# Half of each expert's down product as split operands, and one copy of the whole result

## What is computed

```python
D_MODEL, SEQ, DEPTH = 1024, 512, 2
N_EXPERTS, TOP_K_IN_GROUP, D_EXPERT = 16, 2, 256
for i in range(DEPTH):
    ...
    h = layer_norm_2(DN_ALPHA * h + mix, ln1_g[i], ln1_b[i])
    # two experts of 16 for every token: silu(h @ w1) * (h @ w3) @ w2, weighted by the router
    y_moe = hier_moe(h, moe_wgc[i], moe_bgc[i], moe_wgf[i], moe_bgf[i], moe_w1[i], moe_w3[i], moe_w2[i])
    y_ple = jax.nn.sigmoid(h @ ple_wg[i] + ple_bg[i]) * (p[i] @ ple_wp[i])
    h = layer_norm_2(DN_ALPHA * h + y_moe + y_ple, ln2_g[i], ln2_b[i])
```

## Time and profile before

| | us |
|---|---|
| median of three runs | 3018.23 (3017.04 to 3021.21) |
| the profiled execution, its own time | 3016.39 |
| its span in the trace | 3014.6 |
| PE busy over the span | 2853.4 (95%) |
| DVE busy | 1723.2 (57%) |
| POOL busy | 1538.0 (51%) |
| ACT busy | 1069.8 (35%) |

### The profile page before, as it was taken

The page is one execution under the profiler, slowest core; times in us unless marked ns, Lnnn a source line. Parts: engine busy times, 40 slices in busy tenths (PEclk is TensorE's granted clock), DMA queues, the critical chain, the costliest instruction groups (busy, mean ns, idle before and its releaser), DMA issues. The chain is left out here.

```text
span 3014.6 us, 36257 instructions
## 1 busy us (share of the span) xinstructions
PE 2853.4 (95%) x12934; PEld 2247.6 (75%) x12934; DVE 1723.2 (57%) x2416; ACT 1069.8 (35%) x1851; POOL 1538.0 (51%) x929
## 2 busy tenths in 40 slices
PE   8999999999999999999999999989999799899996
PEld 6778787888876787878888876677667567687774
DVE  5875645443137855554441266566777465667775
ACT  3533323221025333332220122524555314444563
POOL 4543366666764533476666654565225253672241
PEclk9999999999999999999999889999999899899998
DMA  4221122332332211223333222125982321246942
GB/s 150 76 63 56 57 72 83 97 97 94 95 98 70 77 57 50 63 80 95 97 97 106 63 96 64 47 88 188 346 331 106 117 76 50 69 177 232 358 164 84
DMA packets 87034, 338.28 MB, mean 112 GB/s; under 512 B 19952, under 2 KB 22768, under 8 KB 77936
## 3 DMA queue, kind: packets, MB, share of 16 engines
q1 hardware_dynamic: 67744, 303.33, 29.8%
q0 software_dynamic: 17280, 26.26, 2.5%
q10 hardware_dynamic: 1872, 6.82, 0.6%
HBM read 371.98 MB, written 30.41 MB: 133 GB/s over the span
## 5 line engine op out<-in xcount | busy, mean ns | idle before, releaser
L179 POOL TENSOR_SCALAR wh<-ring 128x1024 fp32r<-128x1024 f32 x337 | 371.7, 1103 | 1000.1 <-PE ps L240 779.4
L181 POOL TENSOR_TENSOR wl<-ring,wh 128x1024 fp32r<-128x1024 f32 x337 | 825.6, 2450 | 28.1
L238 PE MATMUL ps<-xh,wh 128*128 128x512 f32 x1720 | 695.4, 404 | 32.7 <-POOL xl L439 11.5
L239 PE MATMUL ps<-xl,wh 128*128 128x512 f32 x1720 | 673.9, 392 | 0.0
L240 PE MATMUL ps<-xh,wl 128*128 128x512 f32 x1720 | 673.9, 392 | 0.0
L238 PEld LDWEIGHTS ps<-xh,wh 128*128 128x128 f32 x1720 | 325.5, 189 | 123.8 <-issue 38.4
L239 PEld LDWEIGHTS ps<-xl,wh 128*128 128x128 f32 x1720 | 326.0, 190 | 70.9 <-issue 6.3
L240 PEld LDWEIGHTS ps<-xh,wl 128*128 128x128 f32 x1720 | 325.3, 189 | 69.6
L1434 DVE SCALAR_TENSOR_TENSOR taps<-ps,par,taps 128x511 f32<-128x511 f32 x192 | 143.9, 749 | 237.0 <-ACT taps L1174 222.2
L2793 DVE TENSOR_TENSOR ew_l<-ew,ew_h 128x1024 fp32r<-128x1024 f32 x184 | 219.2, 1252 | 0.0
L2381 ACT ACTIVATE ew_h<-ew 128x1024 fp32r<-128x1024 f32 x184 | 179.3, 1050 | 0.0
(11 more groups left out here) (501 smaller groups left out, 5161.2 us busy)
## 6 DMA issues: line engine op xcount, KB each, us to landing
ring<-in_w SPq DMA_DIRECT2D x343, 512.0 KB, 3.6
ew<-in_eu SPq DMA_DIRECT2D x32, 2048.0 KB, 9.9
ew<-in_ed SPq DMA_DIRECT2D x32, 1024.0 KB, 9.4
yg<-ypicks SPq DMA_DIRECT2D x16, 512.0 KB, 7.1
xrows<-xr ACTq DMA_DIRECT2D x8, 512.0 KB, 2.6
z<-in_x SPq DMA_DIRECT2D x4, 512.0 KB, 4.5
gw<-in_gw SPq DMA_DIRECT2D x2, 1024.0 KB, 6.5
out<-z SPq DMA_DIRECT2D x8, 256.0 KB, 2.9
```

Source lines behind the costliest of these rows:

```text
L179: nc.gpsimd.tensor_scalar(hi, raw, 1.0, 0.0, ALU.mult, ALU.add).then_inc(sem["w_hi"], 1)
L181: nc.gpsimd.tensor_tensor(lo, raw, hi, ALU.subtract).then_inc(sem["w_split"], 1)
L238: nc.tensor.matmul(out, wh, xh, start=first, stop=False, **kw)
L239: nc.tensor.matmul(out, wh, xl, start=False, stop=False, **kw)
```

## The change

From the third tile of each layer on (`DN_FROM = 2`), the block f = 0 of the down matrix, and the hidden activations that it meets, are split: ACT copies the block's high part into `down_h` (128x1024), DVE subtracts it from the block in place, and DVE also splits the hidden activations into `hidT_h` and `hidT_l` (128x128 each). PE then multiplies that block with `three` instead of with a plain float32 product; block f = 1 stays plain and now comes first. `down_h` is one buffer, so ACT fills it for tile j only when the down product of tile j-1 is finished. The result of a tile, both halves, is now copied by ACT in one instruction of 128x1024, once both banks are finished (`dn_mm`); DVE no longer copies any of it. Only the last tile keeps two copies, both on ACT. On ACT, part 3 of the next tile's high weights now stands ahead of that copy.

```diff
@@ -1468,6 +1468,7 @@
 NOWHERE = 8192
 UP_PARTS = EW_UP // D
 HI_SLOTS = 7
+DN_FROM = 2
 V_POOL = 0
 HY_ORDER = (2, 4, 3, 5, 0, 1)
 HY_EARLY = 4
...
@@ -1571,6 +1572,9 @@
         sil = at_("sil", 152, [P, DE])
         hact = at_("hact", 153, [P, DE])
         hactT = at_("hactT", 154, [P, EC, P])
+        hidT_h = at_("hidT_h", 154, [P, P], F32R)
+        hidT_l = at_("hidT_l", 155, [P, P], F32R)
+        down_h = at_("down_h", 172, [P, D], F32R)
         xr = at_("xr", 156, [P, 4, D])
         xg = at_("xg", 156, [P, 2, D])
         ew_l = at_("ew_l", 80, [P, EW_BUFS, EW_UP + EW_DOWN], F32R)
...
@@ -1613,7 +1617,7 @@
                  "router_ready", "logit_mm", "logits", "route_mm", "r_max", "r_exp", "picks", "rank_mm", "slot_mm", "slots", "spare_ready", "idx_ready", "half_ready2",
                  "rt_in", "xrow_mm", "xrow_evac", "xrow_out", "xg_in0", "xg_in1", "xgt_mm", "xgt_lo", "xgt_hi",
                  "ew_up0", "ew_up1", "ew_up2", "ew_dn0", "ew_dn1", "ew_dn2", "es_up0", "es_up1", "es_dn0", "es_dn1", "e_hi", "e_lo", "up_mm", "silu", "hact", "hactt_mm", "hactt",
-                 "dn_half", "dn_mm", "y_lo", "y_hi", "y_out0", "y_out1", "yg_in0", "yg_in1", "yg_in2", "yg_in3", "zt_mm", "zt_taken",
+                 "dn_half", "dn_mm", "d_hi", "d_lo", "y_done", "y_out0", "y_out1", "yg_in0", "yg_in1", "yg_in2", "yg_in3", "zt_mm", "zt_taken",
                  "tk_mean", "tk_sq", "tk_std", "tk_norm", "xt_mm", "pg_sig", "pp_done", "pt_hi", "pt_lo", "pq_mm", "pq_evac", "stored", "in_rstd", "in_rows", "consts"])
         sem, sem_range = sems(nc, ctx, names)
 
...
@@ -2161,19 +2164,25 @@
                     def expert_down(j):
 
                         b = j % EW_BUFS
-                        pe.wait_ge(sem["hactt"], at("hactt", j + 1))
+                        pe.wait_ge(sem["hactt"], at("hactt", 2 * j + (1 if j >= DN_FROM else 2)))
                         if j < EXPERTS:
                             pe.wait_ge(sem[f"ew_dn{b}"], at(f"ew_dn{b}", 16 * (j // EW_BUFS + 1)))
                         else:
                             k = j - EXPERTS
                             pe.wait_ge(sem[f"es_dn{k % 2}"], at(f"es_dn{k % 2}", 16 * (k // 2 + 1)))
                         if j:
-                            pe.wait_ge(sem["y_lo"], at("y_lo", j))
-                            pe.wait_ge(sem["y_hi"], at("y_hi", j))
+                            pe.wait_ge(sem["y_done"], at("y_done", j))
                         for half in range(2):
-                            for f in range(EC):
-                                a_ = EW_UP + f * D + half * S
-                                mm = T.matmul(ps[:, 5 + half, :], hactT[:, f, :], ew[:, b, a_:a_ + S], start=(f == 0), stop=(f == EC - 1))
+                            a_ = EW_UP + half * S
+                            T.matmul(ps[:, 5 + half, :], hactT[:, 1, :], ew[:, b, a_ + D:a_ + D + S], start=True, stop=False)
+                            if j < DN_FROM:
+                                mm = T.matmul(ps[:, 5 + half, :], hactT[:, 0, :], ew[:, b, a_:a_ + S], start=False, stop=True)
+                            else:
+                                if half == 0:
+                                    pe.wait_ge(sem["hactt"], at("hactt", 2 * j + 2))
+                                    pe.wait_ge(sem["d_lo"], at("d_lo", j - DN_FROM + 1))
+                                mm = three(nc, ps[:, 5 + half, :], hidT_h[:, :], hidT_l[:, :], down_h[:, half * S:half * S + S],
+                                           ew_l[:, b, a_:a_ + S], False, True)
                             mm.then_inc(sem["dn_mm" if half else "dn_half"], 1)
 
                     for j in range(TILES):
...
@@ -2189,9 +2198,7 @@
 
                     for c in range(4):
                         if c == 2:
-                            pe.wait_ge(sem["y_lo"], at("y_lo", TILES))
-                        if c == 3:
-                            pe.wait_ge(sem["y_hi"], at("y_hi", TILES))
+                            pe.wait_ge(sem["y_done"], at("y_done", TILES))
                         for k in range(C8):
                             mm = T.transpose(ps[:, 2 * c + k // 4, k % 4 * P:k % 4 * P + P], z[:, k, c * P:c * P + P], ident)
                         mm.then_inc(sem["zt_mm"], 1)
...
@@ -2389,10 +2396,28 @@
 
                     def y_evac(j):
 
-                        act.wait_ge(sem["dn_half"], at("dn_half", j + 1))
+                        y = y_b if j % 2 else y_a
                         if j >= 2:
                             act.wait_ge(sem[f"y_out{j % 2}"], at(f"y_out{j % 2}", 16 * (j // 2)))
-                        A((y_b if j % 2 else y_a)[:, 0:S], ps[:, 5, :], ACT.Copy).then_inc(sem["y_lo"], 1)
+                        if j == TILES - 1:
+                            act.wait_ge(sem["dn_half"], at("dn_half", j + 1))
+                            A(y[:, 0:S], ps[:, 5, :], ACT.Copy)
+                        act.wait_ge(sem["dn_mm"], at("dn_mm", j + 1))
+                        if j == TILES - 1:
+                            A(y[:, S:2 * S], ps[:, 6, :], ACT.Copy).then_inc(sem["y_done"], 1)
+                        else:
+                            A(y[:, :], ps[:, 5:7, :].rearrange("p a b -> p (a b)"), ACT.Copy).then_inc(sem["y_done"], 1)
+
+                    def down_high(j):
+
+                        b = j % EW_BUFS
+                        if j < EXPERTS:
+                            act.wait_ge(sem[f"ew_dn{b}"], at(f"ew_dn{b}", 16 * (j // EW_BUFS + 1)))
+                        else:
+                            k = j - EXPERTS
+                            act.wait_ge(sem[f"es_dn{k % 2}"], at(f"es_dn{k % 2}", 16 * (k // 2 + 1)))
+                        act.wait_ge(sem["dn_mm"], at("dn_mm", j))
+                        A(down_h[:, :], ew[:, b, EW_UP:EW_UP + D], ACT.Copy).then_inc(sem["d_hi"], 1)
 
                     weights_high(0, range(UP_PARTS))
                     turn_evac(0)
...
@@ -2405,10 +2430,12 @@
                         A(sil[:, :], ps[:, 2 + j % 2, 0:DE], ACT.Silu).then_inc(sem["silu"], 1)
                         if j + 1 < TILES:
                             turn_evac(j + 1)
+                        if j + 1 < TILES:
+                            weights_high(j + 1, (UP_PARTS - 1,))
                         if j:
                             y_evac(j - 1)
-                        if j + 1 < TILES:
-                            weights_high(j + 1, (UP_PARTS - 1,))
+                        if j >= DN_FROM:
+                            down_high(j)
                     y_evac(TILES - 1)
 
                     A(eps[:, 2:3], eps[:, 0:1], ACT.Sqrt)
...
@@ -2816,14 +2843,18 @@
                     def hidden_evac(j):
 
                         dve.wait_ge(sem["hactt_mm"], at("hactt_mm", j + 1))
-                        V.tensor_copy(hactT[:, :, :], ps[:, 4, 0:EC * P].rearrange("p (f t) -> p f t", t=P)).then_inc(sem["hactt"], 1)
-
-                    def y_evac(j):
-
-                        dve.wait_ge(sem["dn_mm"], at("dn_mm", j + 1))
-                        if j >= 2:
-                            dve.wait_ge(sem[f"y_out{j % 2}"], at(f"y_out{j % 2}", 16 * (j // 2)))
-                        V.tensor_copy((y_b if j % 2 else y_a)[:, S:2 * S], ps[:, 6, :]).then_inc(sem["y_hi"], 1)
+                        V.tensor_copy(hactT[:, 1, :], ps[:, 4, P:2 * P]).then_inc(sem["hactt"], 1)
+                        if j < DN_FROM:
+                            V.tensor_copy(hactT[:, 0, :], ps[:, 4, 0:P]).then_inc(sem["hactt"], 1)
+                        else:
+                            do(V.tensor_copy(hidT_h[:, :], ps[:, 4, 0:P]))
+                            V.tensor_tensor(hidT_l[:, :], ps[:, 4, 0:P], hidT_h[:, :], ALU.subtract).then_inc(sem["hactt"], 1)
+
+                    def down_low(j):
+
+                        dve.wait_ge(sem["d_hi"], at("d_hi", j - DN_FROM + 1))
+                        low = slice(EW_UP, EW_UP + D)
+                        V.tensor_tensor(ew_l[:, j % EW_BUFS, low], ew[:, j % EW_BUFS, low], down_h[:, :], ALU.subtract).then_inc(sem["d_lo"], 1)
 
                     dve.wait_ge(sem["xrow_mm"], at("xrow_mm", 8))
                     dve.wait_ge(sem["pp_done"], at("pp_done", C8))
...
@@ -2843,12 +2874,11 @@
                             dve.wait_ge(sem["hactt_mm"], at("hactt_mm", j))
                         V.scalar_tensor_tensor(hact[:, :], sil[:, :], slot_gate[:, j:j + 1], ps[:, 2 + j % 2, DE:2 * DE],
                                                ALU.mult, ALU.mult).then_inc(sem["hact"], 1)
-                        if j:
-                            y_evac(j - 1)
                         if j + 1 < TILES:
                             weights_low(j + 1, (UP_PARTS - 1,))
+                        if j >= DN_FROM:
+                            down_low(j)
                     hidden_evac(TILES - 1)
-                    y_evac(TILES - 1)
 
                     def pick_rows(c):
                         dve.wait_ge(sem["zt_mm"], at("zt_mm", c + 1))

```

(5 more changed lines are left out.)

## The result

The changed kernel takes **3047.79 us** (median of 4 runs, 3046.40 to 3051.12), beside 3017.93 for the kernel before on the same chip: a ratio of 1.010 with an interval of 1.0088 to 1.0112, 29.9 us more. The prediction was slower, 3039.6, between 3022 and 3054. Its sign and its mechanism hold; the size was 8.5 us short, on a predicted difference of 21.4. The profiled execution took 3048.13, its span is 3046.3, against 3014.6 before: 31.7 more.

What follows compares the result with a forecast made beforehand. PE's own work, 10.02 us a tile, bounds the kernel; after the change a closed loop of 10.23 would. Tiles and ends gave 18.2, the clock 3.2: +21.4 on 3016.39, plus 1.8 to the median, 3039.6 us; range 3022 to 3054.

Steps and rivals of the forecast that it cites:

- PE's saving: In the split down product: 0.35 us a tile less, so 9.67 a tile if PE stays the bound.
- rival 5: In the down product: split products miss their pace after the wait, so no 0.35 is won; 3054 us, 4%.
- The loop: From one down product's end to the next through ACT and DVE: 10.23 us, PE waiting about 0.56 a tile.
- the down product, 3.09: Loop term: PE's down product with one block split takes 3.09 us.
- PE's end to the next engine's start, 0.20: Loop term: the next engine starts 0.20 us after PE's product ends, read from DVE's start.
- Residual tiles: Tiles 2 to 6, where DVE also does the residual: 10.95 us against 10.09, +0.86 each.
- rival 3: In residual tiles: the clock falls there as well, ten tiles each 1.7 us longer; 3057 us, 6%.
- The sum over the tiles: Per layer: +0.3 for tile 1, +4.3 for tiles 2 to 6, +2.9 for tiles 7 to 20.
- The ends: In each layer's last tiles: tile 21 -0.5, last tile +2.1 with a 3.8 us wait, half clock +1.6.
- Rival 1: On ACT: the wide copy takes 0.50 us instead of 0.95, the loop 9.78; 3021 us, 8%.
- Rival 2: In the tiles: PE stays the bound, the loop below 9.67 us, tiles gaining 14.3; 3011 us, 5%.
- Rival 4: In iterations 6 and 10, first layer: POOL's split holds up a fifth DVE subtraction, 3044 to 3046 us, 7%.

Runs made afterwards that it cites:

- e1: The changed kernel with the result copied in halves again, the left by ACT after the product's first half, the right by DVE; 3013.0 us, ratio 0.9994.
- e3: The changed kernel with two down_h buffers, their copy ahead of the result's wide copy, split from the fifth tile; 3005.7 us, ratio 0.9966.
- e5: e3 with the result copied in halves on ACT and DVE, as in e1; 3006.4 us, ratio 0.9967.
- e9: e5 with DVE's subtraction of down_h moved ahead of its copy of the result's right half; 2999.3 us, ratio 0.9946.
- e2: The changed kernel with no tile split; only the wide copy on ACT and the new order are kept; 3019.4 us, ratio 1.001.
- after_again: The changed kernel run once more, unedited; 3047.51 us, ratio 1.0103 to the kernel before.
- e4: The changed kernel with the down product split only from the ninth tile of each layer on; 3038.5 us, ratio 1.0074.
- e8: The changed kernel with two down_h buffers, split from the fifth tile, the copy still behind the result's wide copy; 3043.0 us, ratio 1.0091.
- e7: The changed kernel with the last tile's down product of each layer plain again; 3041.9 us, ratio 1.0084.

## Why the prediction was right in sign and short in size

**PE's saving: right.** 0.35 a tile: e1, e3, e5 and e9 all show 9.66 where 9.67 was predicted, as soon as nothing makes PE wait. So rival 5 (split products off their pace) falls.

**The loop: right, 0.14 to 0.16 short.** The step that failed is "the down product, 3.09" with "PE's end to the next engine's start, 0.20". Both were read from a PE that runs without a gap. The same two steps took 3.47. The first half of the product, with its wait ahead, lasts 1.66 (2303.37 to 2305.03), the second about 1.54 (2305.03 to the end of the last split one, 0.23 after 2306.34): a PE that starts from a stand takes 1.13 for its first pair of passes instead of the 1.02 of the second, 0.12 in the half. ACT then starts 0.27 after that end instead of 0.20. This 0.07 isn't the wait's doing: in e3, where PE runs without a gap, ACT's wide copy starts 0.26 after the product's end (last split product 2313.48, plus 0.23, to 2313.97), and in e2's even tiles 0.25. The 0.20 was DVE's, taken for ACT. A forecast of a new wait needs the durations *after a wait*, and the old profile had them: 3.70 for the plain product of the last tile, after a wait of 0.90, beside 3.60 without one.

**Residual tiles.** 11.09 a tile where 10.95 was forecast, the same 0.14; PE waited 1.17 where I had 1.28. The timeline of PE, from one such tile to the next:

```profile
2158.04 1.12 PE L2177 MATMUL ps<-ew,hactT 128*128 128x512 f32 x2 [1.17 <-DVE hactT L2846]
...
2169.13 1.12 PE L2177 MATMUL ps<-ew,hactT 128*128 128x512 f32 x2 [1.17 <-DVE hactT L2846]
```

The product behind them took 1.12, not 1.9, so rival 3 (half clock in these tiles too) falls.

**The sum over the tiles.** Predicted +0.3 + 4.3 + 2.9 = 7.5 a layer up to the last Silu; measured +10.0 and +10.3. Of the 2.6 missing, 19 tiles of 0.14 are 2.7; iteration 6 (16.44 instead of 14.70, twice the forecast 0.86) and iteration 10 (13.40 instead of 14.07, where +0.21 was forecast) cancel. In both layers 5.3 us. That they cancel is luck. PE in iteration 10, in the change and then in after_again:

```profile
2230.76 1.12 PE L2177 MATMUL ps<-ew,hactT 128*128 128x512 f32 x2 [3.45 <-DVE hactT L2846]
```

```profile
2231.65 2.08 PE L2177 MATMUL ps<-ew,hactT 128*128 128x512 f32 x2 [3.45 <-DVE hactT L2846]
```

After the same wait the one product ran at full pace and the other at half, and the iteration took 13.40 and 15.99.

**The ends.** Predicted 2.1 for the last tile and 1.6 for the clock, less 0.5 in tile 21: 6.4 for both layers. The profiles show 12.5 and 10.4 (after_again). What was priced came as priced. The wait is as forecast, 3.36 and 0.38 of transposes, 3.74 against 3.8. The half clock on the last product cost 1.6: from the last transposes to the last split product's start it is 8.36 in the first layer of the change and 6.73 in after_again, at full pace. Behind the second layer's last Silu the change is 3.12 longer, against 3.2. In the first layer the first use of the gathered rows (DVE, `yg`) is 2.95 later than before, counted from the last Silu.

The term that was mis-sized is the one put at nothing: the prediction lets the loss end with the product, and another 6.4 is lost in the stages up to the next layer's first Silu, whose code is unchanged. Windows of the whole stretch, before and then after, show the clock at 0.95 and 0.92:

```profile
2370.00:2720.00 350.00, 320.53 (x1463) 246.57 (x1464) 225.15 (x323) 128.18 (x259) 187.86 (x104) 0.95 0.27 95
```

```profile
2380.00:2740.00 360.00, 326.91 (x1471) 252.12 (x1472) 230.04 (x332) 129.63 (x261) 188.12 (x104) 0.92 0.27 95
```

Whether the last wait brings this on isn't shown, and the executions speak against a fixed price. From the first use of the gathered rows to the next layer's first Silu it is 389.5 before. With a last wait of 3.36 it is 395.9, 395.3, 392.6 and 389.2 (the change, after_again, e4, e8), with one of 1.05 or less 392.6, 392.0, 390.2 and 390.0 (e7, e3, e9, e2). So e8 lost nothing there after the long wait, and e7 lost 3.1 after the short one. The cause stays open.

So the profiled execution's 31.7 is the forecast 21.4, 5.3 more in the tiles and 6.1 more in the ends, less 1.1 in the stretch before them, whose code is unchanged. Between the medians the difference is 29.9.

**The other rivals.** Rival 1 needed a wide copy near 0.50 (its own time, 3021, lies 1 us below the range that was meant to reach it); it is 1.026 by the median of the 22 of one kind, 1.030 at most:

```profile
L2409 ACT ACTIVATE y_a<-ps x22: 1026/1026/1030, 2128.9 to 2994.6; 128x1024 f32<-128x1024 f32 x22
```

The Trainium skill, "VectorE: DVE Perf Modes", section on the TRN2 errata, puts ScalarE's copy out of PSUM below that from SBUF; the direction agrees (1.026 against 1.052), the size is 0.026 instead of its 0.043. In the loop even that is hardly seen: what counts is when the next instruction starts, 0.92 after the wide copy and 0.95 after a copy from SBUF. Rival 2 (PE stays the bound, faster) was refuted for this change, but it is what e3, e5 and e9 do once the loop is opened. Rival 4 (a fifth subtraction caught beside POOL's split) falls. DVE was held up as before and no more: three subtractions took 6.50 instead of 3.49 in iterations 6 and 10, in the change and in after_again, 3.0 longer, where before four took 7.65 instead of 4.62.

```profile
2175.76 6.50 DVE L2820 TENSOR_TENSOR ew_l<-ew,ew_h 128x1024 fp32r<-128x1024 f32 x3
```

What differs from run to run in these iterations is the clock of the product behind the wait, shown above.

## What to carry to other kernels

Before an operation is moved, follow the chain from the end of one product to the start of the next through every queue it passes: an engine with 2.8 us of idle time a tile can still sit in a loop that has none. A second buffer gives nothing while its writer stands behind a waiting instruction in the same queue, and a new order gives little while the buffer is single; try the pair (0.0, 0.2 and 0.7 us a tile here). Look at the last turn of a loop by itself: what other work hides in the middle stands open there, and here it went with the step from a gain of 0.3% (e5) to one of 0.5% (e9), whose intervals overlap a little.

## What the hardware showed beside this

- A wait of PE costs more than its length: the first pair of passes after even 0.46 us of standing took 1.13 instead of 1.02 with the granted clock at 1.00.
- The half clock isn't settled by the length of one wait. A wait of 1.90 was followed by a product of 1.89 in e5, one of 3.36 by 1.36 and then 1.89 in the change (clock 0.53), and one of 3.36 by 1.12 in after_again. In e1 a wait of 2.45 was followed by 1.53 and then 1.72 in the first layer and by 1.13 and then 1.02 in the second. The residual tiles' waits of 1.17 in the change didn't bring it on.
- A fixed stretch of code isn't a fixed time. Up to the first Silu of the expert stage the code is the same in all kernels, and it took 2114.3 to 2118.0 us; so a difference of a few us between two single executions says nothing of an edit.
